# Constant-table products in three waits, a spare power ahead of each norm, an earlier slot load, and x_low moved to VectorE

## What is computed

```python
for l in range(DEPTH):                                   # first stack
    x = layer_norm(ALPHA * x + 0.5 * swiglu(x, ffn1_w_in[l], ffn1_w_out[l]), ...)
    x = layer_norm(ALPHA * x + hybrid_mixer(x, ...), ...)
    x = layer_norm(ALPHA * x + 0.5 * swiglu(x, ffn2_w_in[l], ffn2_w_out[l]), ...)
for i in range(DEPTH):                                   # second stack
    mix = s5_and_pool(x) if i % 2 == 0 else stick_breaking_attention(x @ sb_w_qkv[j]) @ sb_w_out[j]
    x = layer_norm_2(DEEPNORM_ALPHA * x + mix, ...)
    ple = (p[i] @ ple_w_proj[i]) * jax.nn.sigmoid(x @ ple_w_gate[i])
    ffn = grouped_moe(x, router_w, router_bias, moe_w1[i], moe_w3[i], moe_w2[i])
    x = layer_norm_2(DEEPNORM_ALPHA * x + ffn + ple, ...)

def layer_norm(x, g, b):
    mu = jnp.mean(xf, axis=-1, keepdims=True)
    var = jnp.mean(jnp.square(xf - mu), axis=-1, keepdims=True)
    return (xf - mu) * lax.rsqrt(var + LN_EPS) * g + b

def grouped_moe(...):            # each row goes to 2 of 16 experts
    scores = jax.nn.sigmoid(xt @ router_w)
    ...                          # best group of 4 experts, best 2 in it, gates
    h = jax.nn.silu(jnp.einsum('td,edf->etf', xt, w1)) * jnp.einsum('td,edf->etf', xt, w3)
    y = jnp.einsum('etf,efd->td', h * gates, w2)
```

## Time and profile before

| | |
|---|---|
| median of 3 runs | 1750.47 us (1750.35 to 1753.06) |
| profiled execution, its own time | 1750.1 us |
| span, first to last instruction | 1748.4 us |
| mean granted TensorE clock | 0.991 of full speed |
| PE busy | 1679.3 us (96%) |
| DVE busy | 934.4 us (53%) |
| ACT busy | 636.3 us (36%) |
| POOL busy | 117.5 us (7%) |
| chain that ended last | PE 81%, DVE 9%, DMA 5%, ACT 3%, POOL 1%, issue 1% |

### The profile page before, as it was taken

One profiled execution on the slowest core, in us unless ns is written; L12 is line 12 of the kernel. 1 busy time (PEld: TensorE's weight loads), 2 busy tenths in 40 slices (PEclk: granted clock), 3 DMA queues, 4 the chain that ended last, 5 costly groups with the idle time before them and its releaser, 6 DMA issues.

```text
span 1748.4 us, 20780 instructions
## 1 busy us (share of the span) xinstructions
PE 1679.3 (96%) x8496; PEld 1204.8 (69%) x8496; DVE 934.4 (53%) x1317; ACT 636.3 (36%) x826; POOL 117.5 (7%) x91
## 2 busy tenths in 40 slices
PE   8999999999999999999999999999997999999996
PEld 7888877878878888868887787643433777644332
DVE  4754757675465546686686587611114667511114
ACT  4544444354434433443554464211112354211110
POOL 1000060000000000422000000100000000100000
PEclk9999999999999999999999999999999999999998
DMA  7555550655555555515555454799999544799995
GB/s 303 191 189 179 206 172 1 227 182 192 182 191 195 180 190 186 198 49 190 190 191 169 153 216 153 285 429 428 427 427 404 202 145 169 261 426 429 427 427 243
DMA packets 47365, 419.72 MB, mean 240 GB/s; under 512 B 5344, under 2 KB 5344, under 8 KB 9136
## 3 DMA queue, kind: packets, MB, share of 16 engines
q1 hardware_dynamic: 43776, 405.82, 61.0%
q0 software_dynamic: 3504, 12.68, 2.0%
HBM read 417.43 MB, written 1.05 MB: 239 GB/s over the span
## 4 chain that ended last, share of the span: by engine, by line
PE 81%; DVE 9%; DMA 5%; ACT 3%; POOL 1%; issue 1%; DVEq 0%; SPq 0%; POOLq 0%; ACTq 0%
PE hh L1312 11%; PE y L678 10%; PE y L679 10%; PE y L680 10%; PE hh L678 8%; PE hh L680 8%; PE hh L679 8%; DMA wide<-pairs 4%; PE hh L1344 3%; PE turn L1344 3%; DVE w_lo L1940 2%; PE turn L1216 2%; PE y L1355 1%; ACT w_hi L1491 1%; DMA raw<-units 1%; PE turn L798 1%
## 5 line engine op out<-in xcount | busy, mean ns | idle before, releaser
L1940 DVE TENSOR_TENSOR w_lo<-raw,w_hi 128x2048 fp32r<-128x2048 f32 x181 | 411.3, 2290 | 144.2 <-ACT w_hi L1491 143.4
L1491 ACT ACTIVATE w_hi<-raw 128x2048 fp32r<-128x2048 f32 x193 | 365.1, 1912 | 69.9 <-DMA raw<-units 69.7
L678 PE MATMUL hh<-w_hi,xt_hi 128*128 128x512 f32 x704 | 279.0, 396 | 2.0 <-DVE xt_lo L2047 1.1
L680 PE MATMUL hh<-w_hi,xt_lo 128*128 128x512 f32 x704 | 274.6, 390 | 0.0
L679 PE MATMUL hh<-w_lo,xt_hi 128*128 128x512 f32 x704 | 274.2, 389 | 0.0
L678 PE MATMUL y<-w_hi,xt_hi 128*128 128x512 f32 (+1 forms) x464 | 184.1, 397 | 3.4 <-DVE xt_lo L2047 3.1
L680 PE MATMUL y<-w_hi,xt_lo 128*128 128x512 f32 (+1 forms) x464 | 180.0, 388 | 0.0
L679 PE MATMUL y<-w_lo,xt_hi 128*128 128x512 f32 (+1 forms) x464 | 179.9, 388 | 0.0
L1312 PE MATMUL hh<-wide,work 128*64 128x512 f32 x688 | 154.0, 595 | 12.0 <-DMA wide<-pairs 12.0
L678 PEld LDWEIGHTS hh<-w_hi,xt_hi 128*128 128x128 f32 x704 | 132.2, 188 | 30.4 <-DVE xt_lo L2047 2.9
L680 PEld LDWEIGHTS hh<-w_hi,xt_lo 128*128 128x128 f32 x704 | 132.1, 188 | 28.2
(11 more groups left out here) (383 smaller groups left out, 1976.2 us busy)
## 6 DMA issues: line engine op xcount, KB each, us to landing
raw<-units SPq DMA_DIRECT2D x193, 1024.0 KB
wide<-pairs SPq DMA_DIRECT2D x61, 2048.0 KB
extra<-pairs SPq DMA_DIRECT2D x12, 2048.0 KB
xt_wide<-pairs SPq DMA_DIRECT2D x12, 2048.0 KB
wide<-pairs SPq DMA_DIRECT2D x8, 1024.0 KB
late<-pairs SPq DMA_DIRECT2D x5, 1024.0 KB
raw<-pairs SPq DMA_DIRECT2D x5, 1024.0 KB
spare<-pairs SPq DMA_DIRECT2D x2, 2048.0 KB
```

The costliest lines, as they stand in the source:

```text
L678: pe.matmul(dst, left[0], right[0], start=start, stop=False)
L680: return pe.matmul(dst, left[1], right[0], start=False, stop=stop)
L1491: act.activation(hi[r][:, :], raw[r][:, :], ACT.Copy).then_inc(hi_ready, 1)
L1940: dve.tensor_tensor(lo[r][:, :], raw[r][:, :], hi[r][:, :].bitcast(F32), ALU.subtract)\
```

## The change

- SP: `load_wide(0, 1)` is issued behind the load of unit 137 instead of behind that of unit 161; the counted loop is in two parts around it.
- POOL: ahead of each norm's two powers, POOL waits for the first `y_half` (or `moe_part`) of that stage and computes one spare power into a column nobody reads.
- `x_low` is subtracted on DVE, behind `pick_slots(l, 0)` and ahead of `weigh(l, 0, 0)`, instead of on POOL.
- PE: `keep_busy` ahead of `turn_x(0)` in S5 (8), ahead of `turn_x(1)` in `before_experts` (3, both layers), and ahead of `scatter_last(1)` (4, both layers).

```diff
@@ block.sync
-            rounds = BEFORE_MOE[0] // RAW - 2
-            with sp.Fori(0, rounds) as i:
-                for s in range(RAW):
-                    sp.wait_ge(unit_used, i * RAW + s + 1)
-                    sp.dma_start(raw[s][:, :], units(i * RAW + RAW + s)).then_inc(unit_loaded[s], 32)
...
+            def load_rounds(first, last):
+
+                with sp.Fori(0, last - first) as i:
+                    for s in range(RAW):
+                        sp.wait_ge(unit_used, (i + first - 1) * RAW + s + 1)
+                        sp.dma_start(raw[s][:, :], units((i + first) * RAW + s)).then_inc(unit_loaded[s], 32)
+
+            rounds = BEFORE_MOE[0] // RAW
+            load_rounds(1, rounds - 5)
             load_wide(0, 1)
-            for q in range((rounds + 1) * RAW, BEFORE_MOE[0]):
+            load_rounds(rounds - 5, rounds)
+            for q in range(rounds * RAW, BEFORE_MOE[0]):
@@ block.gpsimd
-            def ln_rstd():
+            def ln_rstd(begun, first):
+
                 pool.wait_ge(const_made, 6)
+                pool.wait_ge(begun, first)
+                pool.tensor_tensor(minus_half[:, 2:3], half_pi[:, 0:1], minus_half[:, 0:1], ALU.pow)
                 for t in range(TT):
...
+            def first_y(halves):
+
+                first = seen.ahead(y_half, 1)
+                seen(y_half, halves)
+                return y_half, first
+
             for l in range(DEPTH):
-                ln_rstd()
+                ln_rstd(*first_y(3))
...
-            def low_x(l):
-
-                pool.wait_ge(x_high_ready, l + 1)
-                pool.tensor_tensor(x_low[:, :, :], x[:, :, :], x_high.bitcast(F32), ALU.subtract).then_inc(x_low_ready, 1)
...
-            ln_rstd()
+            ln_rstd(*first_y(2))
             next_ln(a["ln_ffn_g_2"][0], a["ln_ffn_b_2"][0])
-            low_x(0)
-            ln_rstd()
+            first_y(2)
+            ln_rstd(moe_part[0], 1)
...
@@ block.tensor, s5_and_pool
                 four(y_bank[1][0][:, :], w[0], 0, 1, first=False, last=True).then_inc(unit_used, 1)
+                keep_busy(pe, h_bank[0], 8)
                 turn_x(0)
@@ before_experts
                     if u == 0:
+                        keep_busy(pe, h_bank[0], 3)
                         turn_x(1)
@@ gathered_experts
+                keep_busy(pe, gate_bank, 4)
                 scatter_last(1)
@@ block.vector, before_experts
                 pick_slots(l, 0)
+                dve.wait_ge(x_high_ready, l + 1)
+                dve.tensor_tensor(x_low[:, :, :], x[:, :, :], x_high.bitcast(F32), ALU.subtract).then_inc(x_low_ready, 1)
                 weigh(l, 0, 0)
```

More of the change, by code:

```diff
@@ L664, in _ @@
                 pool.memset(fresh[:, :, at:at + 1], 1.0).then_inc(fresh_ready, 1)
-            ln_rstd()
+            ln_rstd(*first_y(2))
             next_ln(a["ln_ffn_g_2"][1], a["ln_ffn_b_2"][1])
-            low_x(1)
-            ln_rstd()
+            ln_rstd(moe_part[1], 1)
             pool.wait_ge(gb_loaded, 2 * 16 * 10)
```

## The result

The changed kernel takes 1735.73 us (median of 6 runs, 1733.40 to 1738.42) against 1751.62 (6 runs, 1747.57 to 1755.36): a ratio of 0.9912, 95% interval 0.9899 to 0.9926. That is 15.9 us less. (The forecast went by the three runs of the kernel before that were known then; the median of all six is 1.2 us higher.) The profiled execution took 1735.64 us with a span of 1733.6, 14.8 less than the span before, at a mean granted clock of 0.995 instead of 0.991. Lines move by up to 13: line 606 is now 614 (611 the spare power), 710 is 718, 1115 is 1123, 1216 is 1225, 1257 is 1267, 2036 is 2047, 2041 is 2052, 2526 is 2537; x_low is line 2562.

The account below looks back on a forecast made before the run. PE was taken as the bound (busy 96% of the span), with DMA at full rate in the experts. 7.4 + 2.8 + 3.2 + 2.2 = 15.6 us off 1750.1 gave 1734.5, or 1734.9 for the median; range 1731 to 1739.5.

Parts of the forecast that it names:

- x_low, 7.4: Routing: subtraction moved to DVE frees the ranking, 4.2 us of PE waits in both layers plus 3.2 of clock in layer 1.
- Spare powers, 2.8: Norms: a spare ahead makes the slow first power as fast as the second; 3.0 us less 0.2 for the scatter.
- only POOL's idle time differs: Norms: argument for the 2.8 us, since DVE starts first beside both slow and fast powers.
- Rival (a): Norms: the port, not idle time, makes the power slow, so spares bring nothing; 3.0 us lost, 1737.9, chance 0.15.
- The slot sooner, 3.2: Start of S5: earlier slot load lets unit 164 land sooner, 1.9 us of wait plus 1.3 of clock.
- the signs that were named: S5: unit 164 landing in under 5 us and line 1115's wait under 0.4 us would show the forecast right.
- Constant products, 2.2: Turn behind S5: eight `keep_busy` calls fill PE's wait and hold the clock, 2.2 us; other groups 0 or 0.2 late.
- Rival (b): Any stage: the clock falls elsewhere, one or two stretches more at 1.7 us each; 1736.6 to 1738.3, chance 0.12.
- (c): S5 doesn't gain, as DVE's scans or the norm's parameter loads replace the wait; 1738.1, chance 0.09.
- (d): Slower: ten waits in experts' tails and one per routing stage bring half clock, 20.4 us; 1755.3, chance 0.02.
- (e): Experts: the load queue, not PE, sets their start, so gains ahead are lost, 0.3 us remain; 1750.2, chance 0.02.
- Gains ahead of the experts survive them: Experts: layer 0's DMA engines stand still 2.5 us ahead, against 2.1 us closed up, so earlier gains should last.

Follow-up runs that it names:

- e2: Changed kernel with the x_low subtraction back on GpSimd: 1741.53 us.
- e1: Changed kernel without the spare powers: 1738.36 us.
- e10: Changed kernel, spare powers kept, with a second wait for the constants put back between spare and first power: 1741.31 us.
- e7: Changed kernel without spare powers, DVE waiting for the norm's power before it multiplies mean and g: 1745.63 us.
- e9: Changed kernel without spare powers, GpSimd's wait for its constants once ahead of the first norm, which keeps both waits: 1735.30 us.
- e3: Changed kernel with the extra slot's load back behind unit 161: 1736.81 us.
- e12: Kernel before the change with one edit, GpSimd's wait for its constants moved once ahead of the first norm: 1748.76 us against 1752.17.
- e4: Changed kernel without the three new groups of constant products (`keep_busy` calls): 1737.54 us.
- e11: Changed kernel with one early power instead of ten spares, the constants' wait ahead of it alone, and three constant products in attention's turn: 1739.28 us.
- e5: Changed kernel with each spare power replaced by a memset behind the same waits: 1736.44 us.
- e6: Changed kernel with the spare powers issued without their wait, so that they run long before: 1734.38 us.

## Why the prediction was right, and where it wasn't

Forecast 1734.9, measured 1735.7; the sum was 15.6 us, the measured difference 15.9, and the ledger's 14.8. That the total comes so near is in part luck: misses up (0.4 twice) and down (0.6 at the slot, 1.0 for a fall of the clock) nearly cancel. Step by step:

- **x_low, 7.4.** Right: 2.3 + 5.5 = 7.8 on the ledger against before, 7.5 when undone alone in e2. The split of the clock's part (all in layer 1) was that of one execution; in e2 it was 1.7 us in each layer (in layer 1, 8.1 us from slot products to gather, against 6.4). x_low on DVE, with 2.29 us, held up no gather: from the slot products to the gather it is 6.4 us in both layers (rows 8: 6.5 at full clock).
- **Spare powers, 2.8.** The size was right (six steps of about 0.5, 3.0 in e1, where the sum had 3.0 less 0.2), the cause was wrong, and so the hit is luck: with a spare in place and one wait more (e10) all nine powers are slow. The step that failed is "only POOL's idle time differs": what also differed was a second wait in front of each first power. Rival (a) had named the port, and its cause holds (e7), but not its result, since it overlooked that the spare power takes the second wait over and brings the start from 0.12 to 0.04 us behind DVE's. What the wait costs is shown by e9 and e10. The evidence was in the code of `ln_rstd` and in the 0.07 us between rows 4 and 5, which I wrote down and put aside. Rows 4 held a second hint: beside an addition from PSUM the power was fast after 240 us.
- **The slot sooner, 3.2.** Mis-sized: 1.6 at the first states against 1.9, and about 1.0 against 1.3 for the clock. Undone alone (e3) it costs 0.9 and no clock, and e12 loads the slot late too and stays at full clock there. So 0.9 to 1.6 us are shown for this edit, and the clock's share isn't. Unit 164 took 5.01 us and the wait was 0.58, both just above the signs that were named (under 5, under 0.4). Moved by 24 units it cost nothing that the ledger shows between 801 and 1012 beyond the norm's 0.5.
- **Constant products, 2.2.** Behind S5 2.6 against before, without the power's 0.5; undone alone (e4) 1.4, where only one stretch fell. The count over 14 traces above says that the products hold the clock, but for e11. Four products ahead of the last scatter cost 0.24 in layer 0 (forecast 0.2) and held no clock up: it is at half at 1343 in the changed kernel, as said.
- **Rival (b)** happened in small: a fall at 753 us, 1.0 us, which the kernel before didn't have in its trace. Since kernels with the same instructions up to there fall or don't, it is no effect of the change that these runs could show.
- **Rivals (c), (d) and (e)** did not happen: S5 gained, none of the 14 traces shows half clock inside the experts, and the gains ahead of the experts came through.
- **Gains ahead of the experts survive them.** Right: 8.9 us ahead of layer 0's, 9.3 behind; 14.9 and 14.8 at layer 1's.

## What to carry to other kernels

When an instruction is long only at its first use in a stage, look at what waits in front of it and at who runs beside it before you blame idle time; a wait that has long been true still costs the start some 0.07 us, and where two engines meet at a port that decides a microsecond. Hoist such waits out of loops, and where it has to hold each time put a small operation with two inputs in GpSimd's queue right ahead of the one that counts (hoisting alone left three of eight powers slow in e9), and take GpSimd off the stretches where VectorE has short operations with two inputs in SBUF. Price a term from a single trace with the clock apart: where it falls differs from one execution to the next.

## What the runs showed of the hardware

The port between GpSimd and VectorE was decided by how late GpSimd comes. Started 0.043 to 0.045 us behind DVE's two-input multiplication, the power took 0.55 us and the multiplication 1.31 instead of 1.28, so neither held the other up; started 0.11 to 0.12 us behind it, the power ended 0.41 to 0.43 us after the multiplication. At 0.05 us it went both ways (e9: 499.87 and 687.55, DVE's multiplication from 499.82 and 687.50). Counted over all 14 traces, with the second powers of the norms: all 196 that started 0.043 to 0.045 us behind that multiplication were fast, 16 of 21 at 0.050 or 0.051, none of three at 0.056 or 0.057, and none of 30 at 0.108 to 0.122. The last norm's first power, 0.11 to 0.12 us behind an addition with one input in PSUM, was fast with two waits as well (0.55 or 0.56 us in before, e1, e7 and e10). The Trainium skill's "SBUF — State Buffer" ("SBUF: two separate sides") says that whichever operation starts first holds the pair for the whole instruction; the trace agrees for late starts and not for the first 0.04 us, where DVE started first and the power wasn't held up. The spare power's own duration shows the same port from the other side: 2.05 us beside DVE's 128x2048 subtraction, 0.56 without it.

With one wait, the start depends on what GpSimd's queue has had since its last subtraction or power. It is 0.043 to 0.045 us behind DVE's where that one stands right ahead, whatever its shape, or where only a memset lies between (twice, in e5's attention norms); 0.050 or 0.051 where the issue of a load or another kind of operation lies between; and 0.056 or 0.057 right behind the issue of the load of p. With two waits it is 0.108 to 0.122. That is what a spare power still gives beyond the wait: it stands right ahead, and in e6 it does so even 246 us before. Which of the 21 at 0.05 us lose was not settled.

The granted clock is no property of the kernel alone. From 289 to 299 us the changed kernel ran at 1.00 and e4 at 0.50 (4.4 us), and both are the same up to there; e7 and e10 have such a stretch of 10.2 us too, at 290.3 and 781.8. At 261 us the clock fell in the changed kernel and not in e3, which is the same up to there.
